# A two-layer encoder with expert lookup on one core: four expert slots of 32 tokens in each gather, products moved among the first gathers, and weight columns written by VectorE

## The reference

```
q = (hb @ w_query).reshape(t, 8 heads, 2, 128)
s = einsum('thpc,phkc->thpk', q, keys); sv, si = top_k(s, 16)
... top 16 of the 256 sums of the two halves -> idx, gate = softmax(top_s)
u = expert_u[idx]                       # t x 128 experts x 1024
act = gelu(einsum('tnd,td->tn', u, hb))
x = x + einsum('tn,tnd->td', gate * act, expert_v[idx])
```

## Time and profile before

| | |
|---|---|
| median of 3 runs | 3069.64 us (3068.76 to 3072.61) |
| profiled execution | 3071.45 us |
| its span, first to last instruction | 3069.7 us |
| busy PE, DVE, POOL, ACT | 85%, 68%, 32%, 19% |
| software DMA queue, 1090.59 MB | 86.6% of 16 engines' span |
| mean granted clock of TensorE | 0.943 |
| first gather issued, last gather issued | 337.81 us, 3045.80 us |

### The profile page before, as it was taken

The page is one execution under the profiler, slowest core; times in us unless marked ns, Lnnn a source line. Parts: engine busy times, 40 slices in busy tenths (PEclk is TensorE's granted clock), DMA queues, the critical chain, the costliest instruction groups (busy, mean ns, idle before and its releaser), DMA issues.

```text
span 3069.7 us, 27540 instructions
## 1 busy us (share of the span) xinstructions
PE 2618.8 (85%) x7006; PEld 1210.0 (39%) x7006; DVE 2096.7 (68%) x6440; ACT 582.0 (19%) x1769; POOL 997.0 (32%) x1107
## 2 busy tenths in 40 slices
PE   9999869897988789778988889888988889877777
PEld 4765424343443334333434334343434334333323
DVE  2143568887778668666788677866877688755555
ACT  2035112111111111112111211121112111111111
POOL 0000033333443333333333333333333333333332
PEclk9999989999999999889999999999998999999899
DMA  5131289999999999999999999999999999999998
GB/s 190 60 130 55 110 330 413 391 395 421 421 421 410 403 421 413 421 414 416 415 408 418 414 407 419 410 414 421 404 410 414 412 416 409 415 408 422 421 421 331
DMA packets 165560, 1139.24 MB, mean 371 GB/s; under 512 B 18672, under 2 KB 19696, under 8 KB 29984
## 3 DMA queue, kind: packets, MB, share of 16 engines
q0 software_dynamic: 149760, 1090.59, 86.6%
q1 hardware_dynamic: 15648, 46.94, 4.0%
HBM read 1135.30 MB, written 2.10 MB: 371 GB/s over the span
## 4 chain that ended last, share of the span: by engine, by line
DMA 50%; PE 33%; DVE 11%; issue 6%; ACT 1%; POOLq 0%; POOL 0%; SPq 0%; DVEq 0%
DMA ring_early<-in_peer_uv,idx_u 17%; DMA ring_early<-in_peer_vu,idx_u 17%; PE psum L1496 16%; DMA ring_late<-in_peer_uv,idx_u 9%; DMA ring_late<-in_peer_vu,idx_u 6%; PE psum L1071 5%; DVE ring_early L1617 4%; PE psum L713 3%; PE psum L755 2%; PE psum L616 2%; DVE ring_late L1617 2%; PE psum L649 1%; DVE work L1188 1%; DVE si L1186 1%; PE psum L578 1%
## 5 line engine op out<-in xcount | busy, mean ns | idle before, releaser
L1496 PE MATMUL psum<-ring_early,w_col 128*128 128x512 f32 x2736 | 1321.4, 626 | 252.3 <-ACT w_col L1559 238.8
L1617 DVE SCALAR_TENSOR_TENSOR ring_early<-ring_early,psum 128x1024 f32<-128x1024 f32 x696 | 846.9, 1217 | 413.5 <-DMA ring_early<-in_peer_uv,idx_u 209.7
L1496 PEld LDWEIGHTS psum<-ring_early,w_col 128*128 128x128 f32 x2736 | 537.3, 201 | 955.5 <-issue 789.5
L1496 PE MATMUL psum<-ring_late,w_col 128*128 128x512 f32 x1360 | 664.9, 628 | 123.3 <-ACT w_col L1559 113.6
L1617 DVE SCALAR_TENSOR_TENSOR ring_late<-ring_late,psum 128x1024 f32<-128x1024 f32 x344 | 418.6, 1217 | 222.9 <-DMA ring_late<-in_peer_uv,idx_u 144.7
L1437 POOL DMA_INDIRECT ring_early<-in_peer_vu,idx_u x348 | 329.2, 946 | 598.2 <-DVE ring_early L1617 285.9
L1437 POOL DMA_INDIRECT ring_early<-in_peer_uv,idx_u x348 | 326.8, 939 | 585.3 <-DVE ring_early L1617 307.7
L1559 ACT ACTIVATE w_col<-ident,weight 128x128 f32<-128x128 f32 x1024 | 343.9, 392 | 644.9 <-DVE weight L1599 638.3
L1496 PEld LDWEIGHTS psum<-ring_late,w_col 128*128 128x128 f32 x1360 | 267.3, 201 | 471.5 <-issue 407.9
L1549 ACT ACTIVATE ge<-ga 128x4 f32<-128x4 f32 (+1 forms) x265 | 54.3, 205 | 1359.7 <-DVE ga L1585 1359.7
L1071 PE MATMUL psum<-wq,hbT 128*128 128x512 f32 x512 | 274.5, 623 | 23.9 <-DVE work L1188 22.8
(11 more groups left out here) (237 smaller groups left out, 1728.9 us busy)
## 6 DMA issues: line engine op xcount, KB each, us to landing
wq<-in_peer_w_query SPq DMA_DIRECT2D x16, 1024.0 KB, 18.0
w_ring<-in_even_w_in SPq DMA_DIRECT2D x5, 2048.0 KB, 8.1
ring_early<-in_peer_vu,idx_u POOLq DMA_INDIRECT x348, 12.9
ring_early<-in_peer_uv,idx_u POOLq DMA_INDIRECT x348, 12.9
w_ring<-in_even_w_out SPq DMA_DIRECT2D x1, 4096.0 KB, 13.9
ring_late<-in_peer_vu,idx_u POOLq DMA_INDIRECT x172, 12.9
ring_late<-in_peer_uv,idx_u POOLq DMA_INDIRECT x172, 12.9
hT<-in_x_T SPq DMA_DIRECT2D x4, 528.0 KB, 7.4
```

What stands on the lines that cost most here:

```text
L1496: ins = nc.tensor.matmul(y_ps[:, half, :], w_col[:, i % W_SLOTS, :], v_cell(at)[:, 512 * half:512 * half + 512], start=False, stop=stop, s ...
L1617: nc.vector.scalar_tensor_tensor(out=cell, in0=cell, scalar=1.0, in1=rows, op0=ALU.mult, op1=ALU.mult, accum_out=dot[par][:, i:i + 1]).the ...
```

## The change

**Layout.** A row of a tile now holds four slots of 32 tokens in place of one slot of 128. Eight rows with the same 32 tokens are a run, and the four blocks of 32 tokens take turns. The weights of a row form a 128 x 32 matrix (`block_fold` times the weight of each partition), and PE adds each row with four products of 256 columns, one in each group of 32 result partitions. The rows that DVE dots with are no longer a copy by ACT: PE repeats the block's 32 tokens four times, in eight products for each run (`fill_tensor`). ACT cuts indices and gates into the new layout with eight small copies each for 16 rows (`stage_u`, `stage_gates`). Results leave PSUM in blocks (`take_blocks`) and a new tile opens block by block (`open_block`). `hb` gets two more buffers.

**Weights.** One DVE operation writes the columns of four rows. ACT keeps the exponentials and no column.

**First gathers.** The first 28 rows use the four early groups only, and POOL's wait for the mixer's end stands behind them. Products 5 to 9 are cut into steps which PE does between the first meta sums; product 3 goes behind the meta scores and product 4 behind the selection of the meta gates. The first two sorts of tile 0's routing are moved in between the meta dots.

```diff
-W_SLOTS = 8
+W_SLOTS = 12
+BLOCK = 32
+RUN = CHUNK // 2
...
-META_ORDER = [0, 1, 2, 3, 0, 1, 2, 3, 4, 5, 0, 1, 2, 3, 4, 5]
...
+EARLY_TILE_ROWS = 12
+EARLY_ROWS = CHUNK + EARLY_TILE_ROWS
+ORDER = ([n % GROUPS_EARLY for n in range(EARLY_ROWS)] +
+         [(GROUPS_EARLY + n) % RING for n in range(2 * XT * TILE_ROWS - EARLY_TILE_ROWS)])
...
+        def fill_tensor(pe, f):
+
+            job, b = f // RUNS + 1, f % BLOCKS
+            pe.wait_ge(s_hb, job + 1)
+            if f:
+                pe.wait_ge(s_dot, CHUNK + RUN * (f - 1))
+            else:
+                pe.wait_ge(s_mix, 2 * XT - 1)
+            for half in range(2):
+                c = slice(512 * half, 512 * half + 512)
+                for g in range(BLOCKS):
+                    nc.tensor.matmul(rows_for((f + 1) % 2)[BLOCK * g:BLOCK * g + BLOCK, c],
+                                     ident[:, BLOCK * b:BLOCK * b + BLOCK], hb_of(job)[:, c],
+                                     start=True, stop=True).then_inc(s_fill, 1)
...
+            for i in range(CHUNK):
+                row = CHUNK * c + i
+                b = row // RUN % BLOCKS
+                if row < RUN * BLOCKS and row % RUN == 0:
+                    open_block(pe, j, b)
+                at = Place(j, row)
                 pe.wait_ge(s_ring[at.group], 16 * (at.uses + 1))
-                pe.wait_ge(s_wcol, CHUNK * u + i + 1)
-                for half in halves:
-                    ins = nc.tensor.matmul(y_ps[:, half, :], w_col[:, i % W_SLOTS, :],
-                                           v_cell(at)[:, 512 * half:512 * half + 512],
-                                           start=False, stop=stop, skip_group_check=True)
...
+                pe.wait_ge(s_wcol, QUADS * number(j, c) + batch(j, c, i)[0] + 1)
+                last = row >= TILE_ROWS - RUN * BLOCKS and row % RUN == RUN - 1
+                for n in range(PARTS):
+                    nc.tensor.matmul(block_part(b, n), w_col[:, at.row % W_SLOTS, :], v_cell(at)[:, part_cols(n)],
+                                     start=False, stop=last, skip_group_check=True).then_inc(s_acc, 1)
...
-                nc.scalar.activation(w_col[:, i % W_SLOTS, 0:cols], base[:, 0:cols], ACT.Copy,
-                                     scale=weight[par][:, i:i + 1]).then_inc(s_wcol, 1)
...
+            wait(dve, s_acc, PARTS * (first + n - W_SLOTS))
+            dve.wait_ge(s_weight, m + 1)
+            nc.vector.tensor_tensor(w_col[:, first % W_SLOTS:first % W_SLOTS + n, 0:width],
+                                    base[:, :].unsqueeze(1).to_broadcast([P, n, width]),
+                                    weight[par][:, x].unsqueeze(2).to_broadcast([P, n, width]), ALU.mult).then_inc(s_wcol, 1)
...
-        META_QUERIED = (7, 23)
-        FIRST_QUERIED = (31, 47, 63, 79)
+        META_QUERIED = (13, 29)
+        SECOND_SORT = 8
+        FIRST_QUERIED = (34, 49, 64, 79)
...
+                    if j == 0 and c == 0:
+                        gather_pool(pool, j, c, range(EARLY_TILE_ROWS))
+                        late_constants(pool)
+                        gather_pool(pool, j, c, range(EARLY_TILE_ROWS, CHUNK))
...
+            products = [(n // 4, lambda n=n: project_step(pe, n)) for n in range(4 * PRODUCT_STEPS)]
+            last = [(10 + n // 2, lambda n=n: project_step(pe, 4 * PRODUCT_STEPS + n)) for n in range(PRODUCT_STEPS)]
+            meta_sums_tensor(pe, products + last + [(8, lambda: fill_tensor(pe, 0)),
+                                                    (CHUNK + RUN - FILL_AHEAD, lambda: fill_tensor(pe, 1))] + of_chunk(early, 0))
```

More of the change, by code:

```diff
@@ L220, in program @@
         spread = sb("spread", [META, P])
-        fold = sb("fold", [P, P])
+        fold = sb("fold", [P, META])
+        block_fold = sb("block_fold", [P, BLOCK])
+        w_col = sb("w_col", [P, W_SLOTS, BLOCK])
+        gate_u = [sb(f"gate_u{i}", [P, CHUNK]) for i in range(2)]
         sel = sb("sel", [P, 2, P])
@@ L756, in project_tensor, with project_step @@
             last.then_inc(s_proj, 1)
+        PRODUCT_STEPS = 1 + KD
+        def project_step(pe, n):
+            i, k = 5 + n // PRODUCT_STEPS, n % PRODUCT_STEPS - 1
+            t, half = PROJECTED[i // 2], i % 2
+            c = slice(512 * half, 512 * half + 512)
+            if k < 0:
+                pe.wait_ge(s_mix, max(i - 3, 2))
+                nc.tensor.matmul(late_bank(i), ident[:, :], hres[:, t, c], start=True, stop=False)
+                return
+            ins = nc.tensor.matmul(late_bank(i), catT[:, k, cols_of(t)], w_out_sb[:, k, c], start=False, stop=(k == KD - 1))
+            if k == KD - 1:
+                ins.then_inc(s_proj, 1)
         def add_projected(dve, i):
@@ L1432, in gather_pool @@
                 if at.summed is not None:
-                    pool.wait_ge(s_acc, at.summed)
-                    if at.summed <= CHUNK:
-                        pool.wait_ge(s_macc, 3 * at.summed)
+                    pool.wait_ge(s_acc, PARTS * at.summed)
                 apart(pool)
@@ L1513, in open_sum @@
[L1513 to L1530 removed]
+            act.wait_ge(s_acc, PARTS * CHUNK)
@@ new lines, in take_meta_sum, with open_block @@
+            for n in range(PARTS):
+                nc.scalar.copy(META_ROWS[:, part_cols(n)], meta_part(n)).then_inc(s_mtaken, 1)
+        def open_block(pe, j, b):
+            if j == 0:
+                pe.wait_ge(s_mtaken, PARTS)
+            else:
+                pe.wait_ge(s_yadd, TAKEN * (j - 1) + TAKEN // 2 * (b // 2 + 1))
+            for n in range(PARTS):
+                nc.tensor.matmul(block_part(b, n), ident[:, block_rows(b)], tile_of(j % XT)[:, part_cols(n)],
+                                 start=(b % 2 == 0), stop=False, skip_group_check=True)
@@ new lines, in take_blocks, with staged_cells @@
+        def take_blocks(eng, copy, j, pair, parts=range(PARTS)):
+            eng.wait_ge(s_acc, PARTS * (CHUNK + TILE_ROWS * j + TILE_ROWS - RUN * 2 * (1 - pair)))
+            for b in (2 * pair, 2 * pair + 1):
+                for n in parts:
+                    copy(hres[block_rows(b), j % XT, part_cols(n)], block_part(b, n)).then_inc(s_yadd, 1)
+        def staged_cells(u, table, staging):
+            c = (u - 1) % TILE_CHUNKS
+            col = P * ((u - 1) // TILE_CHUNKS % 2) + 2 * TOPK * (c // 2)
+            for half in range(2):
+                b = 2 * (c % 2) + half
+                for g in range(BLOCKS):
+                    yield (staging[BLOCK * g:BLOCK * g + BLOCK, RUN * half:RUN * half + RUN],
+                           table[block_rows(b), col + RUN * g:col + RUN * g + RUN])
@@ L1633, in program @@
         LAST = 2 * XT - 1
+        FILL_AHEAD = 12
+        TAKE_AT = 4
         def rows_for(half):
@@ L1846, in _ @@
             add_projected(dve, 2)
-            add_projected(dve, 3)
-            norm_vector(dve, 1, P, tile_of(0), 0)
-            for stage in topk_stages(dve, 0, 0, P, meta=True):
+            for i, stage in enumerate(topk_stages(dve, 0, 0, P, meta=True)):
+                if i == 7:
+                    add_projected(dve, 3)
+                if i == 10:
+                    norm_vector(dve, 1, P, tile_of(0), 0)
                 stage()
@@ L1876, in _ @@
[L1876 to L1881 removed]
+            first = topk_stages(dve, first_piece(1), 0, P)
@@ new lines, in _ @@
+            second = topk_stages(dve, first_piece(1) + 1, 1, P)
+            early = ([(i // 2, first[i]) for i in range(TOPK_STAGES)] + [(7, lambda: piece_indices(dve, 0))] +
+                     [(SECOND_SORT + i, second[i]) for i in range(TOPK_STAGES)] +
+                     [(SECOND_SORT + TOPK_STAGES, lambda: piece_indices(dve, 1))] +
+                     routing_vector(dve, 1, META_QUERIED, 2, piece_indices))
+            dots_vector(dve, None, 0, of_chunk(early, 0) + [(11, lambda: piece_gates(dve, 0))])
```

308 lines of the change are left out of this document (144 added, 164 removed).

## The result

The changed kernel takes 3083.81 us (median of 6 runs, 3082.25 to 3085.28), the kernel before 3069.79 in the same rounds (3067.91 to 3072.61). The ratio is 1.0043, 95% interval 1.0034 to 1.0053: slower by 0.4%, where 3027 was forecast and the range ended at 3060. The profiled executions differ by 10.8 us (3082.25 against 3071.45); the changed kernel's is the fastest of its six, so what follows accounts for 3.2 us less than the medians differ by.

A forecast was written before the change was run, and what follows sets the result against it. PE, falling behind at half clock during queries, was taken to hold up the gathers. From 3071.45, gains of 6.2, 9.1, 23.3, 2.4 and 1.6 gave 3028.9, and 1.8 less for the median 3027 us; range 3002 to 3060.

The forecast's parts named there:

- The failed step: In query rows PE at half clock needs 2.58 us a row against the gathers' 2.486, so it lags.
- the excess: What a stretch takes beyond 2.486 us a gather; 64.8 us behind gather 24 could go.
- The row costs: PE's time a row after the change: 1.83 us with a query piece against 2.58, others 0.65 against 1.72.
- the fourth rival: Slower by the clock: at half clock a query row needs 3.4 us, 3089 us in all; chance 0.03.
- the slack of 7 us: Gathers land 12.9 us after issue in the median, 5.6 at least; a releaser may be 7 us late.
- The dip of 372 GB/s: Tile 3, 1550 to 1570: DMA at 372 GB/s while PE is always busy, read as PE pacing the chain.
- the +3.3 and +0.9 in tiles 1 to 7: Measured changes in us for tiles 1 to 6 and tile 7, where gains of 23.3 and 2.4 were forecast.
- The second rival: DVE takes PE's place in the sorts, each of 28 losing 1.5 to 2.2 us: 3062 us; chance 0.13.
- Tile 0, -9.1 forecast: Tile 0 behind gather 24: of 15.1 us excess 6.0 stay (3.6 for lag, 2.4 for refilling), 9.1 gained.
- The start, -6.2 forecast: Up to gather 24: first gather 5.6 us later, yet the stream ahead by 6.2 us at that gather.
- The end: From the last weight to the end of the last copy: 3.0 us instead of 4.6, gain 1.6.
- The price of the operation: DVE's column operation for four rows: 0.29 us, 0.34 with overlap and waiting, 88 us in all.

The follow-up runs named there:

- number 3: The kernel before with one of the two products of each row's sum left out, except in a tile's last four rows: 3063.01 us, ratio 0.9977.
- number 2: The changed kernel with the weight columns made by ScalarE, one small activation a row, in place of the VectorE operation: 3078.11 us, ratio 1.0025.
- 7: The changed kernel with two copies of 128x1 more on VectorE for each row of tiles 2 to 7: 3096.13 us, ratio 1.0082.
- 9: The changed kernel without three already met waits of VectorE for each batch of four rows, no operation removed: 3079.24 us, ratio 1.0028.
- number 8: The changed kernel with one 128x512 reduction more on VectorE for every four rows of tiles 2 to 7: 3084.86 us, ratio 1.0050.
- Number 1: The changed kernel with the four queries of tile 0 starting 16 rows apart and not 15: 3077.97 us, ratio 1.0027.
- Number 5: The changed kernel with product 4 filling PE's idle time at the start and the meta index selection ahead of the first query: 3074.21 us, ratio 1.0013.

## Why the prediction was wrong

- **The failed step** is "So PE falls behind at half clock and can't catch up before the query ends", taken as the cause of the excess. The row costs were nearly right (a query row without the repetition starts 1.63 to 1.73 us after the last at full clock, where 0.75 + 0.86 = 1.61 was reckoned, and 3.02 at half clock, where the fourth rival's 3.4 less 0.4 for the repetition is 3.0), but a lag of PE costs nothing behind tile 0, since the ring covers it: number 3. The two groups of L1496 in the earlier trace rows are also one row each and not two. I had read the slack of 7 us, and used it for VectorE alone. The windows that answer to the earlier trace rows show what was really there:

```profile
1550.00:1570.00 20.00, 14.22 (x94) 3.98 (x89) 18.96 (x78) 1.96 (x10) 6.63 (x7) 0.82 1.01 406
1640.00:1690.00 50.00, 21.03 (x180) 9.43 (x176) 42.76 (x147) 5.79 (x26) 18.52 (x20) 0.70 1.00 410
```

  The dip of 372 GB/s went with PE and 420 GB/s fell to 410; over both windows together that is 409 GB/s where it was 406, and tiles 1 to 6 got no faster. The dip in the window was not the loss that I took it for.
- **What the excess is.** For the most part VectorE's instruction stream, about 1 us for each 128. This was in no term and no rival. In tiles 3 to 6 the change adds 433 instructions to it, 3.4 fetches: 128 column operations and 128 waits for their weights, which number 2 takes out, but also 128 waits for the gates (`s_gate_u`) and 64 for the repeated rows (`s_fill`), which belong to the layout, less 15 others. That accounts for the +3.3 and +0.9 in tiles 1 to 7, as the steps in tile 7 and numbers 2, 7 and 9 show. The second rival, VectorE's lag in the sorts, isn't the cause: number 8 makes VectorE busy for 107 us more and costs 1.0.
- **The clock.** Its mean fell from 0.943 to 0.776. In tiles 1 to 7 no run shows a loss by that: number 3 had 0.829 and the same time there as before. At the start it cost 2.35 us.
- **Tile 0, -9.1 forecast, +8.7 measured.** I had seen that sorts 15 rows apart make VectorE late (3.6 us), but not who waits for it: PE, at the first piece of the next query, in order ahead of its sums. Number 1 gives 5.8 of it back, without telling PE's wait from VectorE's lag, and number 3 shows that PE's work counts here (gather 144 came 8.0 us earlier). The rest is not taken apart.
- **The start, -6.2 forecast, -1.7 measured.** The order was read rightly, the first gather came at 345.18 instead of 343.4, since the first query took 2.35 us longer than before, at a mean clock of 0.75, and row 24 at 436.94 instead of 434.2. Number 5 shows that 9.6 us lay in the order here: in the 6.41 us for which PE stood idle ahead of the query, in its clock, and in the selection behind it.
- **The end** was right in sign, 0.7 for 1.6. The timeline of the changed kernel, with the last weight and the last copies:

```profile
3073.76 0.16 DVE L1662 TENSOR_TENSOR weight<-gx,ge 128x1 f32<-128x1 f32 x1
...
3075.12 1.80 DVE L1576 COPY hres<-psum 32x256 f32<-32x256 f32 x4 [0.90 <-PE psum L1567]
```

  From the one to the end of the other are 3.2 us where 3.0 was reckoned (4.6 before), but the store and the rest behind it take 3.3 us against 2.4.
- **The price of the operation**, 0.29 us, was right to 1 ns, and it is nearly no part of what it costs.

The Trainium skill, Runtime: NRT & Kernel Launch, Instruction fetch mechanics, says that streams are refilled in blocks of 16 KB or 256 instructions and that the cost is mostly hidden. Here that size fits PE's queue alone (1.75 MB in 107 packets); VectorE's and ScalarE's come in 8 KB, and where gathers fill all DMA engines the cost of VectorE's isn't hidden (0.97 us each in tile 7), so the measurement decides.
